# Expert rows summed one at a time in sixteen 32x32 tiles, with four PSUM banks for the sums and a corrected plan

## The reference

```
q = xs @ wq                                    # 8 heads, two halves of 128
t1, i1 = top_k(q1 . keys1, 16); t2, i2 = top_k(q2 . keys2, 16)
top, j = top_k(t1[:, None] + t2[None, :], 16)  # 16 of 256 pairs
eid = i1 * 128 + i2 at j                       # one of 16384 experts
g = softmax(top)
a = gelu(einsum('nd,nhjd->nhj', xs, u[eid]))
out = einsum('nhj,nhjd->nd', g * a, v[eid])
```

## Time and profile before

| | |
|---|---|
| median of three runs | 3447.25 us (3441.25 to 3448.82) |
| the profiled execution | 3441.62 us, its span 3439.5 us |
| busy, share of span | TensorE 2810.3 us (82%), VectorE 1919.4 (56%), ScalarE 1111.6 (32%), POOL 853.5 (25%) |
| DMA | 1071.76 MB, of it 805.36 by the row gathers; mean 312 GB/s |
| mean granted TensorE clock | 0.895 of full speed |

### The profile page before, as it was taken

One profiled execution on the slowest core, in us unless ns is written; L12 is line 12 of the kernel. 1 busy time (PEld: TensorE's weight loads), 2 busy tenths in 40 slices (PEclk: granted clock), 3 DMA queues, 4 the chain that ended last, 5 costly groups with the idle time before them and its releaser, 6 DMA issues.

```text
span 3439.5 us, 40717 instructions
## 1 busy us (share of the span) xinstructions
PE 2810.3 (82%) x15162; PEld 1750.6 (51%) x15162; DVE 1919.4 (56%) x4582; ACT 1111.6 (32%) x3213; POOL 853.5 (25%) x772
## 2 busy tenths in 40 slices
PE   8999998989888999888775555699999986655555
PEld 6777887655545666564431111278788841211111
DVE  4564764566676556456676766422300256666665
ACT  2232002343574455323533232232310123323222
POOL 0000001234332333223344444200000034444443
PEclk9999999999999999999898776899999987776776
DMA  8264764989998999879999999733144299999998
GB/s 327 99 208 148 289 239 169 369 339 373 373 358 329 417 421 420 336 299 371 404 372 420 415 412 412 308 111 110 57 152 151 73 376 414 411 419 403 411 415 335
DMA packets 151780, 1071.76 MB, mean 312 GB/s; under 512 B 16668, under 2 KB 19356, under 8 KB 23200
## 3 DMA queue, kind: packets, MB, share of 16 engines
q0 software_dynamic: 110592, 805.36, 57.8%
q1 hardware_dynamic: 40992, 263.82, 20.5%
HBM read 1068.06 MB, written 1.05 MB: 311 GB/s over the span
## 4 chain that ended last, share of the span: by engine, by line
PE 51%; DMA 26%; DVE 12%; ACT 6%; issue 3%; POOL 2%; SPq 0%; DVEq 0%; POOLq 0%; ACTq 0%
PE bank L438 38%; DMA ring<-in_experts,eid 25%; PE bank L452 11%; DVE ring L1494 5%; POOL ring L1968 2%; ACT topk_work L1007 1%; ACT topk_work L1000 1%; DMA ring<-in_quads 1%; ACT topk_work L997 1%; ACT L997 1%; DVE state L1729 1%; PE bank L465 1%; PE bank L687 0%; DVE topk_work L1464 0%; PE bank L568 0%
## 5 line engine op out<-in xcount | busy, mean ns | idle before, releaser
L1968 POOL DMA_INDIRECT ring<-in_experts,eid x768 | 853.3, 1111 | 2563.2 <-PE bank L452 1284.2
L452 PE MATMUL bank<-ring,topk_work 64*64 64x512 f32 x6144 | 975.0, 763 | 557.6 <-ACT topk_work L1007 544.3
L1494 DVE CUSTOM_DVE_ANT_0 ring<-ring,h2tok 128x1024 f32<-128x1024 f32 x768 | 937.4, 1225 | 589.1 <-DMA ring<-in_experts,eid 574.9
L452 PEld LDWEIGHTS bank<-ring,topk_work 64*64 64x64 f32 x6144 | 234.7, 158 | 1185.5 <-ACT topk_work L1007 878.3
L997 ACT ACTIVATE topk_work<-topk_work 128x2 f32<-128x2 f32 x384 | 78.0, 203 | 1139.9 <-DVE topk_work L1494 1132.6
L438 PE MATMUL bank<-h_even,weights 128*128 128x256 f32 (+1 forms) x1280 | 293.2, 388 | 4.4 <-ACT h_even L1080 4.0
L438 PEld LDWEIGHTS bank<-h_even,weights 128*128 128x128 f32 (+1 forms) x1280 | 240.9, 190 | 60.8 <-issue 22.8
L438 PE MATMUL bank<-h_odd,weights 128*128 128x256 f32 (+1 forms) x1008 | 228.3, 382 | 0.0
L1007 ACT ACTIVATE topk_work<-const,topk_work 128x64 f32<-128x64 f32 x768 | 225.6, 341 | 0.2 <-ACT topk_work L1000 0.2
L438 PEld LDWEIGHTS bank<-h_odd,weights 128*128 128x128 f32 (+1 forms) x1008 | 187.5, 189 | 49.9 <-issue 23.8
L1000 ACT ACTIVATE topk_work<-topk_work 128x1 f32<-128x1 f32 x768 | 184.6, 287 | 12.6
(11 more groups left out here) (252 smaller groups left out, 3243.6 us busy)
## 6 DMA issues: line engine op xcount, KB each, us to landing
weights<-in_quads SPq DMA_DIRECT2D x151, 1024.0 KB
ring<-in_quads SPq DMA_DIRECT2D x84, 1024.0 KB, 4.9
ring<-in_experts,eid POOLq DMA_INDIRECT x768
weights<-in_quads SPq DMA_DIRECT2D x6, 768.0 KB
ring<-in_quads SPq DMA_DIRECT2D x6, 768.0 KB, 4.5
weights<-in_quads SPq DMA_DIRECT2D x12, 256.0 KB
xT<-in_xT SPq DMA_DIRECT2D x2, 1024.0 KB, 11.7
out<-state SPq DMA_DIRECT2D x4, 256.0 KB, 5.3
```

The source lines that it names most:

```text
L452: x = nc.tensor.matmul(acc[g][out, :], diag[mine, J % 4, :], ring[mine, J % RING, D + h * 512:D + (h + 1) * 512], start=first, stop=J % TI ...
L1494: v.tensor_tensor_reduce(row, row, h2tok[:, u // UNITS % 2, :], 1.0, 0.0, ALU.mult, ALU.add, dots[:, u % 2, j:j + 1]).then_inc(S["dot_done ...
L1968: pool.indirect_dma_start(ring[:, J % RING, :], None, d["experts"], bass.IndirectOffsetOnAxis(eid[:, u % 2, j:j + 1], 0)).then_inc(gathere ...
```

## The change

- `row(J)` takes the place of `row_pair(n)` on the three engines. ScalarE has a Gelu, a multiplication and a diagonal for each row, and starts when that row's dot is done, not the pair's second.
- A row on TensorE is sixteen matmuls of 32x32 tiles: partitions r * 32 and on (r = 0 to 3) times 256 columns c of v, into partitions c * 32 and on of bank `acc[r]`. The diagonal is [128, 32].
- Four banks hold the sums (256 of their 512 columns) and four are left for other jobs, but only from the queries of pass 0 until group 1's rows are over at the end of pass 2, and again from the queries of pass 3 on; in pass 0 and pass 3 before their queries jobs use all eight. `job` remembers who holds a bank, and skips banks whose matmuls are not all issued yet.
- The plan: LAG 5 to 4; a unit of attention counts `UNIT_TAKES` = 2 us more, each of the gates' two halves `GATES_TAKE` = 5 (as a hole that rows may fill), a job of `tile_sum` `SUM_TAKES` = 2; a row counts 0.1 + 0.5 instead of 0.1 + 0.95. Rows are placed one by one; the depths in `rows_before` are doubled, as they count rows (one of them four to four rows, as before).
- Copies of the sums, the last sums, squares, norm and output come in pieces of 256 columns, four parts instead of two; the `turned` jobs have 16 matmuls with 32 columns of output partitions each instead of 8 with 64.
- ScalarE waits before the first decays of linear attention for the eviction of the last gate logits.

```diff
-BANKS = 6
+BANKS, SUMS = 4, 4
-PER_LOAD, LANDS, LAG = 2.5, 2.0, 5.0
+PER_LOAD, LANDS, LAG = 2.5, 2.0, 4.0
+UNIT_TAKES, GATES_TAKE, SUM_TAKES = 2.0, 5.0, 2.0
...
             def job(*key, loose=False):
-                n = len(job_log)
                 job_log.append(key)
-                if n >= BANKS:
-                    pe.wait_ge(*at("evicted", *job_log[n - BANKS]))
+                bank = (cur["bank"] + 1) % cur["banks"]
+                while held.get(bank) in unfinished:
+                    bank = (bank + 1) % cur["banks"]
+                cur["bank"] = bank
+                unfinished.add(key)
+                if bank in held:
+                    pe.wait_ge(*at("evicted", *held[bank]))
+                held[bank], bank_now[key] = key, bank
...
-            def row_pair(n):
-                for J in (2 * n, 2 * n + 1):
-                    k, first = J // TILE_ROWS, J % TILE_ROWS == 0
-                    if first and J:
-                        for g in range(2):
-                            pe.wait_ge(*at("evicted", "acc", k - 1, g))
-                    pe.wait_ge(S["diag_ready"], J + 1)
-                    for h in range(2):
-                        out = slice(h * BLK, (h + 1) * BLK)
-                        for g in range(2):
-                            mine = slice(g * BLK, (g + 1) * BLK)
-                            x = nc.tensor.matmul(acc[g][out, :], diag[mine, J % 4, :],
-                                                 ring[mine, J % RING, D + h * 512:D + (h + 1) * 512],
-                                                 start=first, stop=J % TILE_ROWS == TILE_ROWS - 1, skip_group_check=True)
-                    x.then_inc(S["row_used"], 1)
+            def row(J):
+                k, first = J // TILE_ROWS, J % TILE_ROWS == 0
+                if first:
+                    for r in range(PARTS):
+                        pe.wait_ge(*at("evicted", *held[BANKS + r]))
+                if first:
+                    for r in range(PARTS):
+                        held[BANKS + r] = ("acc", k, r)
+                pe.wait_ge(S["diag_ready"], J + 1)
+                for r in range(PARTS):
+                    mine = part(r)
+                    for c in range(PARTS):
+                        x = nc.tensor.matmul(acc[r][part(c), 0:SPAN], diag[mine, J % 4, :],
+                                             ring[mine, J % RING, D + c * SPAN:D + (c + 1) * SPAN],
+                                             start=first,
+                                             stop=J % TILE_ROWS == TILE_ROWS - 1, skip_group_check=True)
+                x.then_inc(S["row_used"], 1)
...
             def breathe(hole=0.0):
                 end = plan.now + hole
-                while cur["next"] < cur["limit"] and plan.row(2 * cur["next"] + 1) + LAG <= plan.now + hole / 2:
+                while cur["next"] < cur["limit"] and plan.row(cur["next"]) + LAG <= plan.now + hole / 2:
                     emit(cur["next"])
                 plan.now = max(plan.now, end)
...
-                    breathe()
+                    breathe(UNIT_TAKES)
...
-                    breathe()
+                    breathe(GATES_TAKE)
...
             def queries(p):
                 breathe(8.0)
+                cur["banks"] = BANKS
...
                 else:
-                    rows_until(first_pair(p.beside + 1))
+                    rows_until(first_row(p.beside + 1))
                     tile_sum(2 * p.beside + 1)
+                    cur["banks"] = BANKS + SUMS
...
-                act.wait_ge(S["dot_done"], J + 2)
-                nc.scalar.activation(gel[:, m:m + 2], dots[:, par, j:j + 2], ACT.Gelu).then_inc(S["act_gelu"], 1)
-                act.wait_ge(S["act_gelu"], 3 * n + 1)
-                for c in range(2):
-                    nc.scalar.activation(gelw[:, m + c:m + c + 1], gel[:, m + c:m + c + 1], ACT.Copy,
-                                         scale=wts[:, par, j + c:j + c + 1]).then_inc(S["act_gelu"], 1)
+                act.wait_ge(S["dot_done"], J + 1)
+                nc.scalar.activation(gel[:, m:m + 1], dots[:, par, j:j + 1], ACT.Gelu).then_inc(S["act_gelu"], 1)
+                act.wait_ge(S["act_gelu"], 2 * J + 1)
+                nc.scalar.activation(gelw[:, m:m + 1], gel[:, m:m + 1], ACT.Copy, scale=wts[:, par, j:j + 1]).then_inc(
+                    S["act_gelu"], 1)
```

238 lines of the change are left out of this document (130 added, 108 removed).

## The result

The change made the kernel slower. After: 3501.15 us median of 4 runs (3499.79 to 3503.73); before, beside it: 3448.03 (3441.25 to 3450.87). The ratio is 1.0158, 95% interval 1.014 to 1.0175. I had said 3396, with a range to 3465. The profiled execution after has a span of 3499.8 us where before had 3439.5.

What follows compares the result with a forecast made beforehand. No one engine was taken to bound the whole: TensorE held half the chain, expert-row DMA a quarter. Terms -30 - 3 - 9 - 4 - 3 - 2 = -51 us from 3441.62, with the median 5.6 higher, gave 3396; range 3350 to 3465.

Steps and rivals of the forecast that it cites:

- the longer plan times ... put rows earlier among the projections, so that ring slots come free earlier: From 600 to 1150, fewer waits of TensorE for late diagonals: 5 us saved, bounds 0 to 27.
- I credit nothing for those 85/550: Attention, 960 to 1045: no saving counted for some 25 rows, as ScalarE is busy 62 of 85 us.
- 35 us remain: From 600 to 1150: of 41 us less TensorE work at 0.26 a row, 35 us counted as saved on the path.
- the adjoining row: A row on TensorE: two adjoining rows were to cost 0.65 us each, a lone one 0.86.
- My ceiling: The most to gain is the missing DMA share: 54 us from 600 to 1150, 15 us from 1500 to 1800.
- absorbed: Rival, 14%: TensorE's 35 us come back as bank waits (30), table loads and longer attention; 3440 us.
- Starts bound: Rival, 14%: a row's 32 loads and matmuls start no faster than 31 ns apart, a row over 1.055 us; 3492 us.
- The price of a lone row: TensorE's time for a row that stands alone among projections: 0.86 us, with tiles starting 6 ns apart.
- Banks: From 600 to 1150, four banks instead of six cost 10 us, bounds 0 to 30; up to 7 at the gates.
- Stages bound by the DMA: 1800 to 2200 and 2850 to 3420: only bytes count, so 0 us gained, at a lower granted clock.
- the 3 us for eight banks: Stages without rows use all eight banks: 3 us saved, between 0 and 51.
- The end: After the last dot: one row instead of a pair saves 2.5 us, smaller pieces cost 0.5; net 2 saved.

Runs made afterwards that it cites:

- e2_diaglag1: The changed kernel with DIAG_LAG 1 instead of 3, so that ScalarE may take a row earlier: 3442.92 us, ratio 1.0009 to before.
- e9_twice: The changed kernel with DIAG_LAG 1 and each row's sixteen matmuls issued again as a second sweep over all tiles, into unused columns: 3821.28 us, ratio 1.1106.
- e11_lag5: The changed kernel with LAG 5 instead of 4, DIAG_LAG 2 instead of 3 and a row counted at 0.1 + 0.65: 3443.34 us, ratio 1.001.
- e17_load242: The changed kernel with LAG 5, DIAG_LAG 2, a row at 0.1 + 0.65, and PER_LOAD 2.42 instead of 2.5: 3426.71 us, ratio 0.9957.
- e6_fourbanks: The kernel before with the new way to choose banks, only four for jobs beside rows and six elsewhere: 3452.51 us, ratio 1.0035.
- e7_double: The changed kernel with DIAG_LAG 1 and each row's sixteen matmuls issued twice, four by four on the same four tiles: 4061.53 us, ratio 1.1807.
- e16_code: The kernel before with 64 waits already over added on POOL ahead of the wait of every second row: 3492.81 us, ratio 1.0145.

## Why the prediction was wrong, by its steps

**The step that failed** is "the longer plan times ... put rows earlier among the projections, so that ring slots come free earlier", at 5 us saved, together with "I credit nothing for those 85/550" for attention. The 2 us a unit moved rows ahead in TensorE's order and not in ScalarE's, and attention grew by 53 us. I had looked at how busy ScalarE was, and at the earlier trace rows it was busy 62 of 85; the loop needs no full engine. All that was needed stood in the program: two rules for the same row, one changed (5 us after landing to 3) and one not (3 us after landing, by an earlier clock). `e2_diaglag1` shows it: attention back from 161.7 us to 104.9 with the same rows, 51 to 58 us of the total.

**The second** is "35 us remain" as path time. A row's saving was 0.22 us and not 0.26, or 30 us over 136 rows. The term that was off is the adjoining row: I had taken 0.65 us for each of two, and they cost 0.81, while 92 of the 136 rows adjoin another. But TensorE and the DMA were in balance. `e9_twice` shows that an added 0.78 us a row lengthens this stage by 0.64 a row, `e11_lag5` that a saved 0.22 only moves rows out of it, at 2.55 us each. My ceiling had the right quantity in it, the missing DMA share, but I took the share to rise by itself. In these runs it rose only when the plan asked for rows at a higher rate: `e17_load242`, at 3426.7, has 12 of the 51 us. Of the rivals, "absorbed" (3440) comes near to the mended kernels, though not by bank waits; it alone named a longer attention, without saying why it should be longer. Table loads, its other term, are 242 after instead of 232 at 1.28 us each, and 241 in `e2_diaglag1`, so they aren't the cause. "Starts bound" (3492) comes near to the kernel as changed, by luck.

**What held.** The price of a lone row: 0.86 said, 0.83 measured; tiles 7 ns apart, 6 said. "Starts bound" gave the right sign and is false as a cause: it wanted a row over 1.055, and the mean row between 600 and 1150 was 0.83. The Trainium skill, TensorE: Matmul & The Clock Gate, section "Wait — 56ns, not 53.3ns?", has a floor of about 25 ns from start to start of small matmuls. This case's trace doesn't agree, and the measurement decides: the starts came 7 ns apart in a lone row and 17 ns apart in a row that follows another at once. Only the price of a second sweep is near to it, 0.78 us for 32 starts, 24 ns each, in `e9_twice`. Banks: 10 us said, 12 (6 to 18) measured by `e6_fourbanks`, no stage shown for it, and the wait at the gates 7.1 where I had 7; in the kernel after, all waits of TensorE before attention but those for diagonals are 7.2 us. Stages bound by the DMA: no change, at a lower clock. Of the 3 us for eight banks nothing shows.

The end, against the earlier trace rows:

```profile
3486.87 1.22 DVE L1524 CUSTOM_DVE_ANT_0 ring<-ring,h2tok 128x1024 f32<-128x1024 f32 x1 [1.25 <-DMA ring<-in_experts,eid]
...
3488.13 0.20 ACT L1023 ACTIVATE topk_work<-topk_work 128x1 f32<-128x1 f32 x1 [1.54 <-DVE topk_work L1524]
...
3489.13 1.17 PE L470 MATMUL bank<-ring,topk_work 32*32 32x256 f32 x32 [1.32 <-ACT topk_work L1031]
...
3490.47 1.42 DVE L1550 TENSOR_TENSOR dr<-bank,kn_ctx 128x256 f32<-128x256 f32 x4 [2.37 <-PE bank L470]
```

From the last dot to VectorE's first piece 3.60 us instead of 6.04, and from there to the end 9.33 instead of 8.64: 1.7 us saved, 2 said.

## What to carry to other kernels

Where several engines keep their own order of the same units, a change to one engine's rule for when a unit may come has to be held against every other engine's rule: here an order that differs by one place cost a round trip each time, with no engine full. Where two resources are in balance, as TensorE and the DMA were here, a saving on one may pay only when the rate of the other is raised with it; count progress in units of the scarcer one (here rows owed at 2.55 us), or a shorter stage will look like a gain. And try a constant on the old kernel too: 2.42 gains 0.4% with the new rows and loses 0.5% with the old.

## What the runs showed of the hardware

- Matmuls of 32x32 tiles begin 7 ns apart when each goes to another of sixteen tiles, in a lone row of 32 instructions (two sixteens, 0.24 us from one to the other). When a second row follows at once on the same sixteen tiles its starts are 17 ns apart: two rows take 1.62 us in the kernel after where one takes 0.83. A second sweep costs 0.78 us more, not the 0.43 of my estimate for its columns (`e9_twice`), and the same calls given four by four on the same tiles 1.52 us more (`e7_double`, 2.35 against 0.83). The order in which calls go round the tiles counts for as much as their number.
- Some 24,000 waits that were long over (12,000 instructions more in the trace), on the queue that issues indirect gathers, cost 1.5% (`e16_code`), and each gather kept POOL for 1196 ns instead of 1104. The rate from 2850 to 3420 fell from 411 to 397 GB/s.
- With TensorE's row matmuls doubled (127760 instructions, `e9_twice`) the same gathers' packets took 2141 us of the engines' time instead of 1992, and TensorE idled 156.2 us before rows of the last group with nothing in the trace to wait for. What ties these to the instructions is not shown.
